# One 2 MB expert weight load in twenty-four is cut into pieces of 112, 8 and 8 partitions

## The chip, the cores and the metric

One NeuronCore of one Trainium2 chip runs the whole program. The metric is the device time of one execution in microseconds (us). The kernel before takes 1229.42 us, the median of three runs (1229.14 to 1229.61). One more execution was recorded by the hardware profiler; all rows below are from it.

## What is computed

One layer of a hybrid decoder for 256 prompt tokens and 8 sample tokens (264 in all, width 1024, float32), and then a final RMSNorm. The layer has a mixer, a cross-attention into 256 memory tokens, and a mixture of experts (MoE), which takes most of the time:

```
logits = xt @ w_router + b_router
top_logit, top_e = lax.top_k(logits, 4)        # 4 of 32 experts for each token
gates = softmax(top_logit)
def expert_ffn(xb, w1, b1, w2, b2):            # w1: 1024 x 2048, w2: 1024 x 1024, one pair an expert
    gu = xb @ w1 + b1
    gate, up = gu[:, :1024], gu[:, 1024:]
    gate = minimum(gate, 7.0); up = clip(up, -7.0, 7.0)
    return ((up + 1) * gate * sigmoid(1.702 * gate)) @ w2 + b2
out = sum over a token's experts of gates * expert_ffn(token)
```

## The kernel before

**Stages.** A front part (memory keys and values, mixer, attention, router) runs over weight chunks of 1 MB. Then PE, DVE and ACT loop over the 32 experts, eight in one pass of their loop (`it`, `j`; `e = 8 * it + j`). For each expert up to 64 tokens are gathered (`xg`), multiplied by its gate/up weights into two PSUM banks (PE line 1170, 64 matmuls), turned (line 1200), biased and passed through SwiGLU on DVE and ACT (lines 863 to 876, 563), and multiplied by the down weights (line 1217, 32 matmuls). The results are put back to their tokens by a product with the gates (`combine`, lines 1144 and 1145).

**Weights.** An expert has 12.6 MB of weights, loaded as six **units** of 2 MB: units 0 to 3 are gate/up (each two k-tiles of 128 rows by 2048), units 4 and 5 are down. One unit fills two neighbouring slots of `ring`, a buffer of 12 slots of 128 partitions x 2048 floats, so the ring holds exactly one expert's six units. In a unit every partition gets 4096 consecutive floats, 16 KB, of DRAM: this is called a **row** below, and a unit has 128 rows. `unit_slot(i)` gives a unit's first slot; each has a semaphore of its own, `landed[s]`, which every load raises by 16.

**Order.** All weight loads are issued by SP (SyncE), in program order, on one queue (`expert_unit`, line 347). Before it overwrites a unit's slots SP waits until PE has used what was in them: `w_used`, raised by PE behind each unit, or `gu_done` behind unit 3 and `d_done` behind unit 5 (`expert_loads`). SP has nothing else to do in this stage. PE waits on `landed[s]` ahead of each unit's first matmul. SP's loop runs over experts 1 to 31 (`Fori(1, NE)`); expert 0's units were issued ahead of it. A further block repeats all experts if one has more than 64 tokens; it does not run here.

The 16 **DMA engines** move the packets of these loads. The profile gives their mean busy share, not which engine moved what.

Of the kernel before, what the change touches and what calls it, by code (L numbers as in the profile page):

```python
# [21 lines left out]
NE = 32  # L22
# [51 lines left out]
def build(nc, x_t, mem_t, w_k, w_v, w_in, w_out, w_q, w_xo, kc, vc, w_gu, w_dn, params, ws_t,  # L74
# [3 lines left out]
    with ExitStack() as ctx:  # L78
# [3 lines left out]
        def sem(name):  # L82
            return ctx.enter_context(nc.semaphore(name))
# [135 lines left out]
        landed = [sem(f"landed{n}") for n in range(RING)]  # L219
        part_landed = [sem(f"part_landed{n}") for n in range(2)]  # L220
        bias_split = sem("bias_split")
        bias_in = sem("bias_in")
        kv_stored = sem("kv_stored")
        mix_stored = sem("mix_stored")
        y_stored = sem("y_stored")
# [81 lines left out]
        def front_uses(slot):  # L307
            return len(range(slot, NF, RING))

        def unit_slot(i):  # L310

            return (NF + 2 * i) % RING
# [10 lines left out]
        @block.sync  # L323
        def _(sp):
            for part, (k, k_end) in enumerate(FIRST_PARTS):
                sp.dma_start(mem_raw[:, k:k_end, :], mem_t[:, k:k_end, :]).then_inc(mem_in[part], 16)
                sp.dma_start(ring[:, 0, 256 * k:256 * k_end], w_k[0, :, 256 * k:256 * k_end]).then_inc(
                    landed[0] if part == 2 else part_landed[part], 16)
            for n, (kind, c) in enumerate(FRONT_CHUNKS):
                if n == 2:  # L330
                    sp.dma_start(resid[:], x_t).then_inc(x_in, 16)
                if n == 0:
                    continue
                if n >= RING:
                    front_free(sp, n - RING)
                sp.dma_start(ring[:, n % RING, :], front_dram[kind][c]).then_inc(landed[n % RING], 16)

            def expert_unit(e, i):
                s = unit_slot(i)
                dst = ring[:, s:s + 2, :].rearrange("p a n -> p (a n)")  # L340
                if i < 4:
                    rows = w_gu[bass.ds(e, 1), 2 * i:2 * i + 2].rearrange("a k p n -> (a k p) n")
                    src = rows.rearrange("(p j) n -> p (j n)", j=ROWS_GU)
                else:
                    rows = w_dn[bass.ds(e, 1), 4 * (i - 4):4 * (i - 4) + 4].rearrange("a k p n -> (a k p) n")
                    src = rows.rearrange("(p j) n -> p (j n)", j=ROWS_DN)
                sp.dma_start(dst, src).then_inc(landed[s], 16)

            for i in range(UNITS):
                front_free(sp, NF - RING + 2 * i)  # L350
                front_free(sp, NF - RING + 2 * i + 1)
                expert_unit(0, i)

            def expert_loads(e, expert):
                for i in range(UNITS):
                    if i == 3:
                        sp.wait_ge(gu_done, e)
                    elif i == 5:
                        sp.wait_ge(d_done, e)
                    else:  # L360
                        sp.wait_ge(w_used, e * 4 - 3 + min(i, 3))
                    expert_unit(expert, i)

            with sp.Fori(1, NE) as e:
                expert_loads(e, e)

            sp.wait_ge(iters_ready, 1)
            end = sp.value_load(iters[0:1, 0:1], min_val=4, max_val=20)
            with sp.If(end > 4):
                with sp.Fori(1, end >> 2) as again:  # L370
                    with sp.Fori(0, NE) as expert:
                        expert_loads(again * NE + expert, expert)
            for m in range(0, KT, 2):
                sp.wait_ge(y_done, m + 2)
                sp.dma_start(y_t[:, m:m + 2, :], resid[:, m:m + 2, :]).then_inc(y_stored, 16)
            sp.wait_ge(y_stored, 16 * KT // 2)
            sp.wait_ge(kv_stored, 32)
            sp.wait_ge(mix_stored, 48)
# [516 lines left out]
        def _(pe):  # L895
# [252 lines left out]
            with pe.Fori(0, end) as it:  # L1148
                for j in range(8):
                    e, i, cur = it * 8 + j, j % 4, (j // 2) % 2  # L1150
                    twin = it * 4 + j // 2

                    def expert_unit(n):
                        s = unit_slot(n)
                        pe.wait_ge(landed[s], e * 16 + 16 * (front_uses(s) + 1))
                        return ring[:, s:s + 2, :].rearrange("p a n -> p (a n)")


                    pe.wait_ge(gu_copied, e + 1)
                    if i % 2 == 0:  # L1160
                        pe.wait_ge(side_copied, twin * 3 + 1)
                    for u in range(4):
                        if j == 0 and u == 2:
                            pe.wait_ge(emptied, NG)
                        w = expert_unit(u)
                        for k in (2 * u, 2 * u + 1):
                            for n in range(2):
                                for h in range(2):
                                    at = SLOT * (k % 2) + D * h + 512 * n
                                    last = mm(ps[64 * h:64 * h + 64, n, :], xg[:, cur, k, SLOTS * (j % 2):SLOTS * (j % 2) + SLOTS],  # L1170
                                              w[:, at:at + 512], start=(k == 0), stop=(k == KT - 1))
                        last.then_inc(w_used if u < 3 else gu_done, 1)

                    pos = twin * 3 + 2 * (j % 2)
                    if i % 2 == 0:
                        pe.wait_ge(side_copied, pos + 1)
                        pe.wait_ge(w_built, twin + 1)
                        for t in range(TT):
                            width = P if t < 2 else NS
                            last = turn(ps[:, 5, P * t:P * t + width], w_hot[0:width, t, :],  # L1180
                                        ident[0:width, 0:width])
                        last.then_inc(side_filled, 1)
                        pos = pos + 1

                    pair = 1 - i // 2
                    if i == 0:
                        pe.wait_ge(y_copied, twin * 2 + 1)
                    if i == 2:
                        pe.wait_ge(y_copied, twin * 2 + 1)
                    biased = j in (4, 5)  # L1190
                    if j == 4:
                        pe.wait_ge(gates_zero, it + 1)
                    for r in range(2):
                        combine(e * 4, r, 4 * (i % 2) + r, pair, biased)

                    pe.wait_ge(gu_copied, e + 2)
                    pe.wait_ge(t_read, e * 2 + 1)
                    for f in range(KT):
                        first = P * ROWS_DN * (f // ROWS_DN) + f % ROWS_DN
                        last = turn(ps[:, 2 + f // 4, P * (f % 4):P * (f % 4) + P],  # L1200
                                    gu_sb[:, first:first + ROWS_DN * (P - 1) + 1:ROWS_DN], ident[:])
                    last.then_inc(t_done, 1)

                    pe.wait_ge(side_copied, pos + 1)
                    pe.wait_ge(p_built, twin + 2)
                    gather(ps[:, 5, :], j % 2).then_inc(side_filled, 1)
                    for r in range(2, 4):
                        combine(e * 4, r, 4 * (i % 2) + r, pair, biased)

                    pe.wait_ge(hid_ready, e + 1)  # L1210
                    pe.wait_ge(y_copied, e + 1)
                    for u in range(4, UNITS):
                        w = expert_unit(u)
                        for k in range(4 * (u - 4), 4 * (u - 4) + 4):
                            for h in range(2):
                                at = D * (k % 4) + 512 * h
                                last = mm(ps[64 * h:64 * h + 64, 4, :], hid[:, k, :], w[:, at:at + 512],  # L1217
                                          start=(k == 0), stop=(k == KT - 1))
                        last.then_inc(w_used if u < UNITS - 1 else d_done, 1)
# [72 lines left out]
```

## Time and profile before

| | us |
|---|---|
| median of three runs | 1229.42 |
| the profiled execution | 1230.66 |
| its span, first to last instruction | 1228.9 |
| expert stage, about | 277 to 1211 of the span |

The profiled execution is 1.2 us above the median, and 1.8 us of it lie outside the span. A window such as 1196:1201 is in us from the start of the span. "DMA share" is the mean busy share of the 16 DMA engines; a packet is counted where it starts, so a share can pass 1.00 a little. In a chain of waits, each line is the start, the length and what was running or awaited.

### The profile page before, as it was taken

The numbers are of one execution on the slowest core, as the hardware profiler recorded it, in microseconds if no ns is written. First come the engines' busy times: TensorE is split into PE (matmuls) and PEld (weight loads), VectorE is DVE, ScalarE is ACT, GpSimd is POOL, SyncE is SP. The second block draws the span as 40 slices with busy tenths as digits, with TensorE's granted clock in tenths as the row PEclk, the third lists the DMA queues.
The fourth block names the chain that finished last, engine by engine and source line by source line (L and its number), as shares of the span: only waits on it lengthen the run. The fifth ranks groups of instructions, "written<-read, shape, count | busy, mean of one in ns | idle before, by whom it ended". The sixth has DMA issues, their size and how long they took to land.

```text
span 1228.9 us, 14979 instructions
## 1 busy us (share of the span) xinstructions
PE 1162.9 (95%) x5977; PEld 628.8 (51%) x5977; DVE 282.8 (23%) x608; ACT 166.0 (14%) x267; POOL 31.9 (3%) x68
## 2 busy tenths in 40 slices
PE   8999999999999999999999999999999899999995
PEld 7888887784444454444344434443444343434443
DVE  5114532342111122121111111111111111111115
ACT  2011011022111111111111111111111111111112
POOL 0000000010000000000000000000000000000000
PEclk9999999999999999999999999999999999999998
DMA  9963434948999999999999999999999999999991
GB/s 365 387 222 138 139 138 175 429 189 331 431 426 428 428 427 427 426 427 427 429 427 427 428 427 428 427 428 427 429 427 428 426 428 427 427 429 427 429 397 57
DMA packets 38703, 458.87 MB, mean 373 GB/s; under 512 B 5841, under 2 KB 6353, under 8 KB 7921
## 3 DMA queue, kind: packets, MB, share of 16 engines
q1 hardware_dynamic: 35712, 454.11, 88.1%
q10 hardware_dynamic: 2928, 3.80, 0.9%
q8 instruction: 54, 0.88, 0.3%
q14 instruction: 9, 0.07, 0.0%
HBM read 454.41 MB, written 3.23 MB: 372 GB/s over the span
## 4 chain that ended last, share of the span: by engine, by line
DMA 44%; PE 29%; DVE 3%; issue 1%; DVEq 0%; ACT 0%; SPq 0%; ACTq 0%
DMA ring<-in_w_gu 44%; PE ps L1170 19%; PE ps L1217 6%; PE ps L1145 1%; DVE arena L863 1%; PE ps L1200 1%; PE ps L1117 1%; DVE arena L873 1%; DVE arena L876 1%; PE ps L1144 0%; DVE arena L870 0%; DVE resid L890 0%; DVE resid L882 0%; DVE ssum L608 0%; PE ps L1180 0%
## 5 line engine op out<-in xcount | busy, mean ns | idle before, releaser
L1170 PE MATMUL ps<-ring,arena 128*64 128x512 f32 x2048 | 457.5, 599 | 36.7 <-DMA ring<-in_w_gu 29.2
L1170 PEld LDWEIGHTS ps<-ring,arena 128*64 128x64 f32 x2048 | 144.9, 138 | 343.8 <-issue 279.4
L1217 PE MATMUL ps<-ring,arena 128*64 128x512 f32 x1024 | 226.8, 595 | 6.3 <-DVE arena L876 6.3
L842 DVE TENSOR_TENSOR resid<-resid,ps 128x264 f32<-128x264 f32 x128 | 51.3, 426 | 722.4 <-PE ps L1145 722.4
L940 PE MATMUL ps<-arena,ring 128*128 128x264 f32 (+1 forms) x800 | 179.2, 386 | 1.4 <-issue 1.0
L940 PEld LDWEIGHTS ps<-arena,ring 128*128 128x128 f32 x800 | 151.6, 190 | 27.3 <-issue 1.6
L1217 PEld LDWEIGHTS ps<-ring,arena 128*64 128x64 f32 x1024 | 70.7, 137 | 146.9 <-issue 130.7
L1117 PE MATMUL ps<-arena 128*128 128x128 f32 x816 | 101.7, 281 | 0.0
L1117 PEld LDWEIGHTS ps<-arena 128*128 128x128 f32 x816 | 99.1, 197 | 0.0
L555 ACT ACTIVATE arena<-ps 128x1024 f32<-128x1024 f32 x32 | 32.8, 1024 | 446.2 <-PE ps L1170 446.2
L1145 PE MATMUL ps<-arena 128*128 128x264 f32 x256 | 72.6, 396 | 0.0
L569 ACT ACTIVATE arena<-ps 64x512 f32<-64x512 f32 x32 | 18.9, 590 | 249.4 <-PE ps L1217 249.4
L1145 PEld LDWEIGHTS ps<-arena 128*128 128x128 f32 x256 | 44.8, 190 | 15.2 <-issue 9.7
L863 DVE TENSOR_TENSOR arena<-ps,par 128x512 f32<-128x512 f32 x64 | 44.0, 688 | 25.9 <-PE ps L1200 25.9
L1200 PEld LDWEIGHTS ps<-ident,arena 128*128 128x128 f32 x256 | 34.7, 207 | 7.4 <-issue 6.3
L1200 PE MATMUL ps<-ident,arena 128*128 128x128 f32 x256 | 36.9, 287 | 1.4
L431 POOL TENSOR_TENSOR arena<-arena,gate 128x384 f32<-128x384 f32 x17 | 14.2, 833 | 879.1 <-PE ps L1180 873.0
L563 ACT ACTIVATE arena<-arena 128x512 f32<-128x512 f32 x32 | 20.2, 630 | 85.2 <-DVE arena L868 85.2
L967 PE MATMUL ps<-ring,arena 128*128 128x256 f32 x128 | 28.0, 379 | 0.0
L967 PEld LDWEIGHTS ps<-ring,arena 128*128 128x128 f32 x128 | 24.3, 190 | 3.3
L876 DVE TENSOR_TENSOR arena<-arena 128x512 f32<-128x512 f32 x32 | 22.2, 692 | 3.3
L565 ACT ACTIVATE arena<-ps 128x512 f32<-128x512 f32 x32 | 19.1, 597 | 27.6 <-PE ps L1117 27.6
(187 smaller groups left out, 433.5 us busy)
## 6 DMA issues: line engine op xcount, KB each, us to landing
ring<-in_w_gu SPq DMA_DIRECT2D x128, 2048.0 KB, 23.8
ring<-in_w_dn SPq DMA_DIRECT2D x64, 2048.0 KB, 20.4
ring<-in_w_in SPq DMA_DIRECT2D x10, 1024.0 KB, 27.2
ring<-in_kc SPq DMA_DIRECT2D x8, 1024.0 KB, 4.7
ring<-in_vc SPq DMA_DIRECT2D x8, 1024.0 KB, 4.8
ring<-in_w_v SPq DMA_DIRECT2D x4, 1024.0 KB, 22.7
ring<-in_w_out SPq DMA_DIRECT2D x4, 1024.0 KB, 4.9
ring<-in_w_q SPq DMA_DIRECT2D x4, 1024.0 KB, 4.8
```

Source lines behind the costliest of these rows:

```text
L555: nc.scalar.activation(gu_sb.rearrange("p (a b) -> p a b", a=2), ps[:, 0:2, :], ACT.Copy).then_inc(gu_copied, 1)
L563: nc.scalar.activation(sig[:], tb[:, :, 0:SLOTS], ACT.Sigmoid, scale=ALPHA).then_inc(sig_ready, 1)
L842: TTN(resid[:, m, :], resid[:, m, :], ps[:, 6 + m % 2, 0:T], ALU.add).then_inc(c_added, 1)
L863: TTN(both[:, :, h, :].rearrange("p (b m) s -> p b m s", b=2), turned[:, :, h, :].rearrange("p (b m) s -> p b m s", b=2), bc(bias, 3, [P, ...
L876: TTN(hid[:], up_v, sig[:], ALU.mult).then_inc(hid_ready, 1)
L940: last = mm(b[:, 0:width], w[:, k, P * (m % 2):P * (m % 2) + P], source(k), start=(k == 0), stop=(k == KT - 1))
L967: last = mm(b[:, 0:256], mem[:, k, P * t:P * t + P], w[:, k, :], start=(k == 0), stop=(k == KT - 1))
L1117: last = mm(b[:, P * part:P * part + P], h_tok[:, t, first:first + ROWS_GU * (P - 1) + 1:ROWS_GU], p_hot[:, t, :], start=(t == 0), stop=(t ...
L1145: mm(ps[:, 6 + m % 2, 0:T], y_hot[:, pair, P * m:P * m + P], g_hot[:, pair, :], start=not biased, stop=True).then_inc(c_filled, 1)
L1170: last = mm(ps[64 * h:64 * h + 64, n, :], xg[:, cur, k, SLOTS * (j % 2):SLOTS * (j % 2) + SLOTS], w[:, at:at + 512], start=(k == 0), stop= ...
L1200: last = turn(ps[:, 2 + f // 4, P * (f % 4):P * (f % 4) + P], gu_sb[:, first:first + ROWS_DN * (P - 1) + 1:ROWS_DN], ident[:])
L1217: last = mm(ps[64 * h:64 * h + 64, 4, :], hid[:, k, :], w[:, at:at + 512], start=(k == 0), stop=(k == KT - 1))
```

## The change

SP's first unit of experts 1, 5, 9, ..., 29 (eight units of 192) is no longer one transfer of 128 partitions. It goes out as rows 112 to 119, then rows 120 to 127, then rows 0 to 111. The two small transfers raise a new semaphore, `tilt_landed`, by 16 each; the large one raises `landed[s]` as before. PE, ahead of the first unit of every expert with `i == 1` (`j` 1 and 5), now waits on `landed[s]` and on `tilt_landed`. The bytes, their source and their place in SBUF are the same. To tell the experts apart SP's loop now covers four experts a pass (seven passes, experts 1 to 28) and three experts are written out behind it.

```diff
-            def expert_unit(e, i):
+            def expert_unit(e, i, uneven=False):
...
-                sp.dma_start(dst, src).then_inc(landed[s], 16)
+                if not uneven:
+                    sp.dma_start(dst, src).then_inc(landed[s], 16)
+                    return
+                for p in (112, 120):
+                    sp.dma_start(dst[p:p + 8], src[p:p + 8]).then_inc(tilt_landed, 16)
+                sp.dma_start(dst[0:112], src[0:112]).then_inc(landed[s], 16)
...
-                    expert_unit(expert, i)
-
-            with sp.Fori(1, NE) as e:
-                expert_loads(e, e)
+                    expert_unit(expert, i, quarter == 1 and i == 0)
+
+            with sp.Fori(0, NE // 4 - 1) as quad:
+                for i in range(1, 5):
+                    expert_loads(quad * 4 + i, quad * 4 + i, i)
+            for e in range(NE - 3, NE):
+                expert_loads(e, e, e % 4)
...
                         w = expert_unit(u)
+                        if i == 1 and u == 0:
+                            pe.wait_ge(tilt_landed, quad * 32 + 32)
```

On SP, at the top of the loop over experts, the kernel before has this for the first two units (`w_used` is PE's count of used units):

```order
L364 ISA
L347 ISA [waits w_used]
L347 DMA ring<-in_w_gu 128x4096
L361 REGISTER_ALU
L347 ISA [waits w_used]
L347 DMA ring<-in_w_gu 128x4096
```

The kernel after has this in the same place, for the first expert of the four in a pass:

```order
L370 ISA
L352 ISA [waits w_used]
L352 DMA ring<-in_w_gu 8x4096
L352 ISA
L352 DMA ring<-in_w_gu 8x4096
L353 REGISTER_ALU
L353 DMA ring<-in_w_gu 112x4096
L367 REGISTER_ALU
L349 ISA [waits w_used]
L349 DMA ring<-in_w_gu 128x4096
```

One DMA has become three behind the same wait; the next unit follows as before.

On PE, at the start of the gate/up matmuls of an expert with `i == 1`, before (the last matmuls of the expert ahead, then the first unit; `landed8` belongs to the last down unit, `landed10` to the first gate/up unit):

```order
L1217 MATMUL ps<-ring,arena 64x512 [waits landed8]
...
L1170 MATMUL ps<-ring,arena 64x512 [waits landed10]
L1170 MATMUL ps<-ring,arena 64x512 x7
```

and after:

```order
L1229 MATMUL ps<-ring,arena 64x512 [waits landed8]
...
L1165 ISA [waits gu_copied]
L1177 ISA [waits landed10]
L1182 MATMUL ps<-ring,arena 64x512 [waits tilt_landed]
```

The wait on `landed10` has moved to an instruction of its own, and the matmul carries the new wait. ACT, DVE and GpSimd run the same instructions in the same order.

## Rows read from the trace of the kernel before

**Rows 1.** The page's second part: each line in 40 slices of the span.

```profile
PE   8999999999999999999999999999999899999995
DMA  9963434948999999999999999999999999999991
GB/s 365 387 222 138 139 138 175 429 189 331 431 426 428 428 427 427 426 427 427 429 427 427 428 427 428 427 428 427 429 427 428 426 428 427 427 429 427 429 397 57
```

**Rows 2.** Chain that ended last: start us, length us, what; its middle and end.

```profile
600.46 3.68 PE ps L1170 x16
604.30 25.57 DMA ring<-in_w_gu
629.91 3.68 PE ps L1170 x16
633.76 25.99 DMA ring<-in_w_gu
659.79 3.68 PE ps L1170 x16
...
1162.99 3.68 PE ps L1170 x16
1166.83 26.14 DMA ring<-in_w_gu
1203.06 7.11 PE ps L1217 x32
```

**Rows 3.** DMA view of 290:1203, the stretch in which the queue is never empty.

```profile
DMA packets 26613, 387.51 MB, mean 424 GB/s; under 512 B 2960, under 2 KB 2960, under 8 KB 2960
q1 hardware_dynamic: 26567, 386.79, 99.7%
q8 instruction: 42, 0.69, 0.3%
```

**Rows 4.** Windows at the end of the last load: length, PEclk, DMA share, GB/s.

```profile
1192.00:1192.50 0.50, 1.00 1.00 426
1192.50:1193.00 0.50, 1.00 0.85 360
1193.00:1193.50 0.50, 1.00 0.92 393
1193.50:1194.00 0.50, 1.00 0.77 328
1194.00:1194.50 0.50, 1.00 0.62 262
1194.50:1195.00 0.50, 1.00 0.69 295
1195.00:1195.50 0.50, 1.00 0.38 164
1195.50:1196.00 0.50, 1.00 0.46 197
1196.00:1201.00 5.00, 1.00 0.51 216
1201.00:1201.50 0.50, 1.00 0.22 66
1201.50:1202.00 0.50, 1.00 0.08 33
```

**Rows 5.** DMA view of 1200:1203: GB/s in 40 slices of 0.075 us; the fetch queue.

```profile
GB/s 437 218 0 0 437 218 437 0 437 218 0 0 218 219 219 0 219 0 0 0 0 0 218 0 0 0 0 0 0 0 0 0 0 0 0 0 0 0 0 0
q8 instruction: 1, 0.02, 2.3%
```

**Rows 6.** DMA issues of the page: form, count, KB each, median us to landing.

```profile
ring<-in_w_gu SPq DMA_DIRECT2D x128, 2048.0 KB, 23.8
```

**Rows 7.** Timeline of SP, the last two groups of issues of weight loads.

```profile
1155.45 11.71 SPq L347 DMA_DIRECT2D ring<-in_w_gu  x4
1177.00 3.77 SPq L347 DMA_DIRECT2D ring<-in_w_dn  x2
```

**Rows 8.** DMA view of 269:272, slices of 0.075 us: one load into 32 partitions.

```profile
GB/s 0 0 0 0 0 0 0 0 0 0 0 0 218 382 273 0 0 55 546 273 1 0 0 0 0 0 0 0 0 0 0 0 0 0 0 0 0 0 0 0
q10 hardware_dynamic: 48, 0.13, 18.6%
```

More of the change, by code:

```diff
@@ L222, in build @@
         bias_in = sem("bias_in")
+        tilt_landed = sem("tilt_landed")
         kv_stored = sem("kv_stored")
@@ L352, in _, with expert_loads @@
                 expert_unit(0, i)
-            def expert_loads(e, expert):
+            def expert_loads(e, expert, quarter):
                 for i in range(UNITS):
@@ L370, in _ @@
                 with sp.Fori(1, end >> 2) as again:
-                    with sp.Fori(0, NE) as expert:
-                        expert_loads(again * NE + expert, expert)
+                    with sp.Fori(0, NE // 4) as quad:
+                        for i in range(4):
+                            expert_loads(again * NE + quad * 4 + i, quad * 4 + i, i)
             for m in range(0, KT, 2):
@@ L1150, in _ @@
                     e, i, cur = it * 8 + j, j % 4, (j // 2) % 2
-                    twin = it * 4 + j // 2
+                    twin, quad = it * 4 + j // 2, it * 2 + j // 4
                     def expert_unit(n):
```

## Prediction

> **What bounds the kernel now.** I read the slices of the page first. From the eleventh slice on the DMA line stands at 9, and the rate at 425 to 431 GB/s up to the 38th slice [rows 1]. PE is busy too, so the chain of waits has to decide. In it a long wait for a gate/up load comes once an expert, followed by 16 matmuls of 3.7 us, and the loads take the rest of each period [rows 2]. From 600.46 to 1162.99 there are 19 experts: 29.61 us each. PE is the follower; what arrives last sets the period.
>
> What does an expert need at the mean rate? Six units of 2.097 MB at 427 GB/s are 29.47 us, 4.91 us a unit. The period is 0.14 us longer. The mean rate is that of 16 engines; the period is that of the engine that ends last, since a unit counts as landed only when its last row is there. So the engines are not level, and fall further apart with every expert.
>
> The end of the last load shows how far. After SP's last issue (1177.00 to 1180.8, [rows 7]) no work is added, so each engine runs dry when its own backlog ends. The share falls from 1.00 at 1192 to 0.46 at 1196, and then stands at 0.51 for five whole microseconds, until it falls to nothing at 1201 to 1202 [rows 4]. Half of 16 is eight: **eight engines are done by about 1195, and eight work on for some seven microseconds more.** The mean gap follows from the areas. From 1192 to 1196 the shares sum to 2.85 us, times 16 is 45.5 engine-us; the late eight take 32 of them, so the early eight stop 1.7 us behind 1192, at 1193.7 on average. Behind 1201 there are (0.22 + 0.08) x 0.5 x 16 = 2.4 engine-us left, of which a fetch has 1.1 [rows 5]: the late eight stop at about 1201.2. The gap is 7.5 us.
>
> Where does it come from? Beside the weights there is one other queue in that stretch, instruction fetches: 42 packets of 16 KB [rows 3], each of which holds an engine for 2.3% of 16 x 3 us = 1.1 us [rows 5]. If only the late eight carry them, that is 5.25 each; 7.5 us of gap would be 1.4 us a fetch, a little over its own 1.1 us. The order of size fits. Which engine takes them no row says.
>
> **The change part by part.**
>
> (1) *What an uneven unit does to the engines.* A row of 16 KB is one packet: 26613 packets less the 2960 small ones, over 387.51 MB, are 16.4 KB each [rows 3]. A unit is 128 rows on 16 engines, 8 each, so a row costs its engine 4.91 / 8 = 0.614 us. The piece of 112 gives 7 rows to each engine. A piece of 8 rows is 8 packets, so at most eight engines get one. If both pieces go to the same eight, these carry 9 rows and the others 7: one row, 0.614 us, moves from one half to the other. The Trainium skill, "DMA: Bandwidth & Descriptors", section "Why a DMA increments its semaphore by 16 and not by 1", says that a transfer of SP runs on the largest number of engines up to 16 that divides its slowest dimension, and on the lowest-numbered ones; by it both pieces would use one and the same half. No transfer in this trace has so few rows, so no row bears it out.
>
> (2) *Sum over the run.* Eight such units: 8 x 0.614 = 4.9 us off one half and onto the other. All eight fall into the stretch with a full queue, so nothing evens it out in between.
>
> (3) *Is 4.9 us the right amount?* Now the single engines count, not the means. The last row of the late half starts in the slice at 1201.65 [rows 5] and ends at 1202.3. The early half's last row: the share at 1194.5 to 1195.0 is 0.69, so it still has work there, and at 1195.0 to 1195.5 it has none [rows 4]; I take 1195.4 for its end. With the late half lightened: 1202.3 - 4.9 = 1197.4. The early half becomes 1195.4 + 4.9 = 1200.3, and is last. **The gain is 1202.3 - 1200.3 = 2.0 us.** The swap is overdone; the ideal would be half of 6.9. That no time comes of the other 2.9 us is what is late next.
>
> (4) *Does PE get it?* The chain ends with the last expert's unit 3 (1166.83 + 26.14 = 1192.97), then PE, DVE and ACT until 1203.06, where the down matmuls begin [rows 2]. Units 4 and 5 have landed by then, at the latest by 1202.3 and some tenths. The chain waits for unit 3's last row, which the same late engine brings, and so moves by the same 2.0 us.
>
> (5) *What is added.* SP issues two DMAs more eight times. A load lands a median 23.8 us behind its issue [rows 6], which is 23.8 / 4.91 = 4.8 units: the queue is nearly five units deep and covers it. If that cover were gone, two issues would cost well under 1 us, eight times. Behind SP's waiting instruction only later loads are queued. PE gets one instruction more on eight experts, at a unit whose rows stand ahead of the one the chain waits for: nothing. Small packets for the semaphores are among the 2960 that leave a unit at 4.91 us: 0.1 us in all. SP's longer program may bring two or three fetches; if they go where the others go, the late half has 2.9 us of new slack: nothing. Sum: -2.0 + 0.1 = -1.9 us, a span of 1227.0, 1228.8 for the profiled execution, and **1227.5 us** against the median.
>
> **The rivals.**
>
> *A (forecast), load shift off the late half:* 1227.5, with 1226.0 to 1229.0 as its own range: the early end is read to 0.4 us, and a fetch more or less on the last engine is 1.4 us.
>
> *B, the wrong half.* The pieces fall on the eight engines that are late already. They decide from the first uneven unit on: +4.9 us, **1234.3**. The trace says that exactly eight are late; nothing says which. Speaking against B: nothing in a row, so it keeps a real chance.
>
> *C, the pieces collide on their way into SBUF.* Each of 16 engines brings 427 / 16 = 26.7 GB/s, all at once, into 128 partitions. If neighbouring partitions share a way in that passes no more than one engine's stream, eight engines that write into eight neighbours at once are slowed: through two such ways a piece takes 4 x 0.614 = 2.46 us in place of 0.61, +1.84 us. An engine takes its rows in order, so its later rows wait too. Sixteen pieces: +29.5 us on one half, which has 2.0 us to spare after the shift: +27.5 us, 1257. The large piece also no longer lies as whole units do; at the worst it would take its 4.9 us twice, eight times, another 39 us: 1296. I take 1275. It decides from 2.0 / 8 = 0.25 us a unit on: a little collision suffices to eat the gain. For it: the one load into 32 partitions moves its 0.13 MB in the eight slices from 269.9 to 270.5, 218 GB/s, about half of 427 [rows 8]. Against it: part of these 0.6 us is the first packet's latency, and single slices reach 382 and 546 GB/s, far more than a limit of half would let through if it bit at once. So a buffer or no limit; I cannot tell. The Trainium skill, "SBUF — State Buffer", section "Door 1: The DMA port swizzle", says that 16 ports serve 128 partitions, and that bandwidth depends on how many of them the partitions reach; by it four engines would write through one port, and this change would be slower. That is rule C, and it speaks against the change; rows 8 agree with it in the mean and not in the peak.
>
> *D, nothing is shifted.* The small pieces go alternately to the two halves, or the late engines are late by position in the queue and not by load: 1229.4.
>
> **How the numbers follow.** A 0.50, B 0.10, C 0.34, D 0.06. A's mechanism is read from the share of 0.51 and needs one free choice (the half) and the absence of C; C has half of rows 8 for it. The bound of 0.2% is 2.5 us, about what a measurement of this kernel can tell from no change: faster is below 1227.0, slower above 1231.9. A's 1.9 us is inside it, and passes it in about a quarter of A. Faster 0.13; same 0.37 + 0.06 = 0.43; slower 0.10 + 0.34 = 0.44. The range runs from 1226.0 up to where C is half covered, 1272: some 0.03 below and 0.16 above it.
>
> **What would show it.** A: after SP's last issue, the plateau of about half share shrinks from five microseconds to two or three (the means would be 1196.3 and 1198.6), and the mean period of an expert is 29.54 instead of 29.61 us. The mean rate stays at 427. B: the plateau grows to some 15 us. C: the share stays near 1 while the rate falls below 427 GB/s behind each first unit of experts 1, 5, 9, ..., since packets take longer. D: rows 4 come again. The size would be wrong if a fetch costs other than 1.4 us or if the number of fetches changes by more than two.

## The result and the profile after

The kernel after takes **1324.58 us** (median of four runs, 1319.51 to 1327.86), the kernel before 1229.51 beside it: a ratio of 1.077, interval 1.0753 to 1.0787, or +95.1 us. The forecast was 1227.5 with a range to 1272. The profiled execution has a span of 1322.8 us.

The page's second part, against [rows 1]: PE's and the DMA engines' busy tenths, the granted TensorE clock, and the rate, in 40 slices of 33 us.

```profile
PE   9999999999998998799969987998899878978995
...
PEclk9999999999999999899989998999899989999998
DMA  9863437769999999999999999999999999999981
GB/s 372 342 223 129 143 144 315 309 190 427 429 427 331 428 428 422 301 428 428 386 310 420 427 384 329 397 424 379 327 397 422 382 363 399 408 363 362 379 364 39
```

The DMA line is at 9 as before, so the engines are still called busy. But the rate, 425 to 431 before, dips every fourth slice: 331, 301, 310, 329, 327, and from there it hardly comes back. The dips have the spacing of the cut units.

Windows of SP (length, PEclk, DMA share, GB/s) around the cut unit of expert 13, issued at 646.6:

```profile
645.00:650.00 5.00, 1.00 0.99 419
650.00:655.00 5.00, 1.00 1.07 429
655.00:660.00 5.00, 1.00 1.00 216
660.00:665.00 5.00, 1.00 1.04 210
665.00:670.00 5.00, 1.00 0.99 177
670.00:675.00 5.00, 0.83 1.01 239
675.00:680.00 5.00, 0.50 0.97 301
680.00:685.00 5.00, 0.99 1.01 390
```

For 20 us all 16 engines are busy (share 1.00) and move half of what they moved before (177 to 239 for 427 GB/s). Busy and half as fast: their packets take twice as long. No engine runs dry in these 20 us; what is slow is the packets themselves.

The chain of waits, start and length, against [rows 2]:

```profile
600.37 25.47 DMA ring<-in_w_gu
625.88 3.68 PE ps L1182 x16
629.71 25.59 DMA ring<-in_w_gu
655.35 3.68 PE ps L1182 x16
659.17 42.11 DMA ring<-in_w_gu
701.33 3.68 PE ps L1182 x16
...
793.91 6.49 PE ps L1182 x16
```

Experts without a cut unit wait 25.5 us as before; the one with it waits 42.11, 17 us more. That is the longest. The long waits behind the other cut units are 34.37, 38.30, 34.40, 33.51, 34.93 and 31.70, and from 734 on the waits next to these are longer too (27 to 31 us). The last line is a second cost. Inside the long wait PE runs out of work, from 670.64 to 676.71. Its granted clock falls to 0.83 and then to 0.50 (1.2 GHz, 675:680 above), and the 16 down matmuls behind that gap take 5.33 us for 3.65. Where such a stretch meets the chain, 16 matmuls that took 3.68 us take 6.49, 6.19 and 5.78, 7.4 us more together.

The DMA view of 290:1300, against [rows 3]:

```profile
DMA packets 26826, 388.90 MB, mean 385 GB/s; under 512 B 3088, under 2 KB 3088, under 8 KB 3088
...
q1 hardware_dynamic: 26780, 388.18, 97.6%
q8 instruction: 42, 0.69, 0.3%
```

The bytes are the same, 388 MB, in 1010 us instead of 913. Fetches are the same 42, so SP's longer program brought none. The weight queue fills 97.6% instead of 99.7%, which with the fetches leaves some 21 us of the 1010 in which the engines, on the mean, have no work. Most of these lie at the end: from 1284 to 1300 the share is 0.09, and from 1286 to 1296 it is 0.07, one engine of 16 that works on alone where [rows 4] had eight. The rest of the loss is mostly slower packets, with some stretches in which engines run dry (1240 to 1250, share 0.70). The large pieces land a median 35 us behind their issue, where [rows 6] has 23.8:

```profile
ring<-in_w_gu SPq DMA_DIRECT2D x120, 2048.0 KB, 25.5
ring<-in_w_gu SPq DMA_DIRECT2D x8, 1792.0 KB, 35.0
```

### The profile page after: what moved, and what is told of

It reads as the page before. It is cut to its first block, busy times and chain, and to the rows that moved or that the text cites. A ratio compares the mean times of both kernels' runs of the same rounds, so it can differ in the third digit from the quotient of the medians.

```text
span 1322.8 us, 14938 instructions
## 1 busy us (share of the span) xinstructions
PE 1185.6 (90%) x5977; PEld 631.0 (48%) x5977; DVE 282.6 (21%) x608; ACT 165.9 (13%) x267; POOL 31.8 (2%) x68
## 4 chain that ended last, share of the span: by engine, by line
DMA 61%; PE 16%; DVE 2%; issue 1%; ACT 0%; SPq 0%; DVEq 0%; ACTq 0%
DMA ring<-in_w_gu 61%; PE ps L1182 13%; PE ps L1229 2%; PE ps L1127 0%; DVE arena L873 0%; PE ps L1212 0%; PE ps L1155 0%; DVE resid L900 0%; DVE arena L883 0%; DVE arena L886 0%; DVE resid L892 0%; DVE ssum L618 0%; DVE rstd L626 0%; DVE arena L880 0%; SPq L349 0%
## 5 line engine op out<-in xcount | busy, mean ns | idle before, releaser
L1182 PE MATMUL ps<-ring,arena 128*64 128x512 f32 x2048 | 475.0, 614 | 100.0 <-DMA ring<-in_w_gu 94.2
L1229 PE MATMUL ps<-ring,arena 128*64 128x512 f32 x1024 | 230.8, 603 | 15.8 <-DMA ring<-in_w_dn 9.6
## 6 DMA issues: line engine op xcount, KB each, us to landing
ring<-in_w_gu SPq DMA_DIRECT2D x120, 2048.0 KB, 25.5
```

## The experiments

The theory to be tested is rival C of the prediction: rows collide on their way into SBUF. Its rivals are the number of transfers, SP's new loop, the load moved onto late engines (rival B), and a pattern in DRAM. All kernels are edits of the kernel after, with PE's wait on `tilt_landed` set to what their loads raise. Each time is set against the kernel before as it ran beside it (medians of 1229.25 to 1229.65 us).

### Not the loop, not the count: c1_loop_only and c2_columns

```diff
-                for p in (112, 120):
-                    sp.dma_start(dst[p:p + 8], src[p:p + 8]).then_inc(tilt_landed, 16)
-                sp.dma_start(dst[0:112], src[0:112]).then_inc(landed[s], 16)
+                sp.dma_start(dst, src).then_inc(landed[s], 16)     # c1; and PE's new wait taken out
```

> The kernel after, with its SP loop over four experts, but every unit is again one transfer of 128 partitions and PE has no new wait. Ways-in theory (neighbouring partitions share a way into SBUF, and a piece whose rows go to few of these ways slows every engine that writes there): nothing collides, 1229.5 us. Count theory (the cost is in the number of transfers, semaphores and issues of SP): 1229.5 us too. Loop theory (SP's longer program or its fetches cost the 95 us): 1324 us. So this run bears on the loop alone.

Measured 1229.22 us, ratio 0.9997 (0.9988 to 1.0007). The loop costs nothing.

```diff
+                for c in (3584, 3840):
+                    sp.dma_start(dst[:, c:c + 256], src[:, c:c + 256]).then_inc(tilt_landed, 16)
+                sp.dma_start(dst[:, 0:3584], src[:, 0:3584]).then_inc(landed[s], 16)
```

> The kernel after, but the same eight units are cut along the free dimension: 128 partitions x 3584 floats, and twice 128 partitions x 256 floats, with the same bytes in each piece (1792, 128, 128 KB), the same semaphores and the same waits. Ways-in theory: every piece reaches all ways as a whole unit does, so 1229.5 to 1231 us. Count theory: three transfers in place of one cost what they cost in the kernel after, 1324 us.

Measured 1230.97 us, 1.0009 (1.0000 to 1.0019), 1.6 us more. Three transfers with the same bytes, semaphores and waits as in the change are nearly free when each covers 128 partitions. Forecast term (5) had 0.1 us for what is added. The small pieces have rows of 1 KB here and of 16 KB in the change, so the 1.6 us is not exactly its term, but either is of no weight beside 95.

### Not the moved load: c3_112_16 and c4_64_64

```diff
+                sp.dma_start(dst[112:128], src[112:128]).then_inc(tilt_landed, 16)    # c4: [64:128]
+                sp.dma_start(dst[0:112], src[0:112]).then_inc(landed[s], 16)          # c4: [0:64]
```

> The kernel after, but the eight units are cut into 112 partitions and 16 partitions, so that all 16 engines should carry 7 + 1 rows, as many as in a whole unit: no load moves from one half of the engines to the other. Wrong-half theory (the 95 us are rows moved onto late engines): 1229.5 us. Ways-in theory: the 16 rows go through few ways and the 112 rows do not lie on the engines as a whole unit's do, so most of the loss stays, 1270 to 1320 us.

Measured 1308.73 us, 1.0647 (1.0619 to 1.0675).

> The kernel after, but the eight units are cut into two halves of 64 partitions, 4 rows for each engine and half. Wrong-half theory: no load moves, 1229.5 us. Ways-in theory: each half reaches only half of the ways if they go by blocks of partitions, so a unit takes up to 4.9 us more, eight times: up to 1269 us; less than in the kernel after, since each way still has only two writers.

Measured 1320.97 us, 1.0753 (1.0717 to 1.0789). Each piece has a multiple of 16 rows. If these are dealt out evenly, which no row shows engine by engine, no engine gets more than another, and nearly the whole loss is there. So it is not the load, for which rival B had only 4.9 us in any case. But the size of c4 is a miss: 39 us were expected, 91.6 came. The window of its cut unit of expert 13 shows why the sum fell short; the stretch of half rate is 20 us long, though the unit itself at half rate would take 9.8:

```profile
655.00:675.00 20.00, 0.96 1.00 214
```

### Large piece or small pieces: d1_only_112 and d2_only_8s

One leaves out rows 112 to 127 of the eight units, the other rows 0 to 111.

```diff
+                sp.dma_start(dst[0:112], src[0:112]).then_inc(landed[s], 16)                # d1, nothing else
+                sp.dma_start(dst[112:120], src[112:120]).then_inc(tilt_landed, 16)          # d2
+                sp.dma_start(dst[120:128], src[120:128]).then_inc(landed[s], 16)            # d2
```

> The eight units load only partitions 0 to 111; rows 112 to 127 are left out (PE multiplies what lay there before). Small-piece theory (the cost is in the two pieces of 8 rows, four engines at one way): without them 8 x 0.614 = 4.9 us less than before, 1224.5 us. Large-piece theory (the 112 rows do not lie on the engines as a whole unit's do, and engines meet at ways all along): most of the 95 us stay, 1270 to 1310 us.

Measured 1305.94 us, 1.0621 (1.0569 to 1.0674), +76.6 us: the large piece alone carries most of the 95 us. By rows alone the run would have taken 4.9 us less than the kernel before, so the surplus is 81.5 us, 10.2 a unit. The rate around its cut unit of expert 13 (650 to 665) is 203, 190 and 170 GB/s at a share of 0.98 to 1.04, the same picture as above.

> The eight units load only the two pieces of 8 rows; rows 0 to 111 are left out. If small pieces cost only their rows (2 x 0.614 us on eight engines, in place of 8 x 0.614 on all): some 30 us less than before, 1195 to 1200 us. If four rows in a row share one way: 2 x 2.46 = 4.9 us a unit, as much as a whole unit, 1229 us. If the small pieces carry the 95 us: 1290 us or more.

Measured 1230.06 us, 1.0005 (0.9995 to 1.0016), as the middle case said. Two pieces of 8 rows, an eighth of the bytes, keep the engine that ends last as long as a whole unit of 128 rows. Both parts of C's sum are seen here apart: the small pieces had been priced right (4.9 us a unit), the large one was the part that was taken for an uncertain extra.

### Only the place in SBUF changed: d3_extra_contig and d4_extra_step4

The units are whole again; two further pieces of 8 rows go to spare space, from the same source rows.

```diff
+                spare = arena[:, h_at:h_at + 2048]
+                for p in (0, 8):                                                            # d3
+                    sp.dma_start(spare[p:p + 8], src[p:p + 8, 0:2048]).then_inc(tilt_landed, 16)
+                for p in (0, 1):                                                            # d4
+                    sp.dma_start(spare[p:p + 29:4], src[8 * p:8 * p + 8, 0:2048]).then_inc(tilt_landed, 16)
                 sp.dma_start(dst, src).then_inc(landed[s], 16)
```

> The eight units are whole again (128 partitions); ahead of each, two more pieces of 8 rows x 2048 floats are loaded from the same unit into spare space, one into partitions 0 to 7, one into 8 to 15. Ways-in theory: eight engines write into two groups of four partitions, 4 x 0.307 us a piece; 16 pieces are 19.7 us for these engines, of which 6.9 us are slack if they are the early half: 1242 us (1249 if they are the late half), more if others are held up with them. If only rows count: 16 x 0.307 = 4.9 us, hidden in the early half (1229.4) or not in the late half (1234.3).

Measured 1241.23 us, 1.0098 (1.0082 to 1.0115), +11.9 us: beside the 1242 of the ways-in theory. That figure held for eight early engines, though, and the next run says that two of the eight are late. With a late one among them the same sum gives 1249. So a piece with 8 KB a row costs a late engine about 11.9 / 16 = 0.74 us here, not 1.23. That is still more than its rows (0.31), but that the time came out beside 1242 is in part luck, and the size stays open.

> As the run with contiguous extra pieces, with the same source rows and bytes, but the 8 rows go to every fourth partition: 0, 4, ... 28, and then 1, 5, ... 29, so that each row lies in a group of four partitions of its own. Ways-in theory: no two engines meet, so only the rows count: 1229.4 us if the eight engines of such a piece are the early half, 1234.3 us if they are the late half, and so this run also tells which half the small pieces of the change load. Source theory (the loss comes from how rows are read from DRAM): the same time as with contiguous partitions.

Measured 1233.77 us, 1.0035 (1.0023 to 1.0048). The same bytes from the same rows by the same number of transfers are 7.5 us cheaper when every row goes to a group of four partitions of its own. And the 4.4 us that are left speak of the second question, which engines a piece of 8 rows loads. The end of its last load, in windows of SP, against [rows 4]:

```profile
1194.00:1196.00 2.00, 1.00 0.92 393
1196.00:1198.00 2.00, 1.00 0.86 369
1198.00:1200.00 2.00, 1.00 0.59 254
1200.00:1201.00 1.00, 1.00 0.62 262
1201.00:1204.00 3.00, 1.00 0.19 76
1204.00:1205.00 1.00, 1.00 0.12 49
```

Before, eight engines (0.51) worked on by themselves for five microseconds. Here the share at 1196 is 0.86: most of the early half has been loaded and goes on. But at the end two engines are alone (0.12 of 16), and they end the load. That is what one sees if the eight engines of such a piece are neither the early half nor the late one, but about six early and two late ones. d2 ends in the same way: two engines alone from 1192.5 to 1196 (share 0.13). No single row names an engine, so the numbers six and two are read from the shares.

### Destination or source: f3_even_odd, g1_dst_blocks, g2_src_blocks

```diff
+                sp.dma_start(dst[1:128:2], src[1:128:2]).then_inc(tilt_landed, 16)          # f3
+                sp.dma_start(dst[0:127:2], src[0:127:2]).then_inc(landed[s], 16)            # f3
```

> The eight units are cut into the 64 odd partitions and the 64 even ones, 4 rows for each engine and half as in the run with two blocks of 64, which took 1321 us. Ways-in theory: each half now reaches every group of four partitions and so every way, and two engines that meet alternate between two ways: 1240 to 1270 us. Source or shape theory (any transfer of fewer than 128 partitions is slow, wherever its rows go): 1321 us again.

Measured 1229.80 us, 1.0001 (0.9991 to 1.0011). Two halves of 64 partitions cost 91.6 us as blocks and nothing as odd and even ones. Better than expected, and by itself not a proof, as the source rows changed with the partitions. The next two part them; g1 has `dst[64:128] <- src[1:128:2]` and `dst[0:64] <- src[0:127:2]`, g2 has `dst[1:128:2] <- src[64:128]` and `dst[0:127:2] <- src[0:64]`.

> The eight units are cut into two halves of 64 rows; the odd rows of DRAM go to partitions 64 to 127, the even rows to 0 to 63 (so PE multiplies permuted weights in these units). Destination as in the run with two blocks of 64 (1321 us), source as in the run with odd and even rows (1230 us). Ways-in theory (the loss arises where the rows enter SBUF): 1321 us. Source theory (it arises in the pattern in which rows are read from DRAM): 1230 us.

Measured 1318.29 us, 1.0716 (1.0669 to 1.0763).

> The counterpart: rows 64 to 127 of DRAM go to the odd partitions, rows 0 to 63 to the even ones (permuted weights again). Source as in the run with two blocks of 64 (1321 us), destination as in the run with odd and even rows (1230 us). Ways-in theory: 1230 us. Source theory: 1321 us.

Measured 1229.23 us, 0.9998 (0.9986 to 1.0009). The page's rates in 40 slices show the two side by side, g1:

```profile
GB/s 372 341 226 130 135 153 307 310 190 427 426 428 336 427 428 427 317 428 428 397 330 427 427 366 345 427 427 346 347 428 428 331 320 428 425 338 307 420 375 42
```

and g2:

```profile
GB/s 369 391 215 138 139 137 188 427 178 342 429 426 428 429 427 426 425 427 430 427 428 427 428 427 427 427 429 427 427 427 429 426 427 428 427 428 427 428 401 61
```

For these halves the partitions written decide, not the rows read. The Trainium skill, "SBUF — State Buffer", section "Door 1: The DMA port swizzle", gives the map: 16 ports, two groups of four neighbouring partitions to a port, and the two halves of 64 partitions on different ports. A block of 64 reaches half the ports, the odd partitions reach all. The trace agrees: half the rate (214 GB/s, c4) with blocks, 427 without.

The swap was made for halves of 64 only. By the same map a block of 112 reaches every port, so counting ports does not explain the 76.6 us of d1. That there, too, several engines write through one port at a time fits the same signature (share near 1, rate near 200 GB/s), but no run took source and place apart for that piece.

### A price that grows: f1_first_only and f2_last_only

In the seven units that are not cut, SP loads the whole unit and raises `tilt_landed` by 32 itself. In f1 the loads of experts 1 to 4 are also written out ahead of SP's loop.

```diff
+                if uneven == 2:
+                    sp.sem_inc(tilt_landed, 32)
-                if not uneven:
+                if uneven in (0, 2):
```

> Only the first of the eight units (expert 1) is cut into 112, 8 and 8 partitions; the other seven are whole. Fixed-price theory: each cut unit costs 95 / 8 = 11.9 us, so 1241 us. Skew theory (a cut unit slows all engines for as long as some engine is still in it, so its price grows with how far the engines have drifted apart, and at expert 1 they have drifted by about 1 us only): the dip in the rate there is worth some 3 to 4 us in the trace of the kernel after, so 1232 to 1234 us.

Measured 1233.66 us, 1.0034 (1.0021 to 1.0047): +4.0 us. From 262 to 310 us the DMA engines moved 12.28 MB here and 13.65 MB in the kernel before. The difference is 3.2 us of the full rate, most of the price.

> Only the last of the eight units (expert 29) is cut; the other seven are whole. Fixed-price theory: 1241 us. Skew theory: the engines are 8 us apart there as in the kernel before, so more than at expert 1: 1240 to 1244 us. The difference between this run and the run with the first unit alone is what tells the two theories apart: none by fixed price, 8 us or so by skew.

Measured 1244.04 us, 1.0119 (1.0102 to 1.0136): +14.4 us. The same cut costs 4 us at expert 1, where by the skew theory the engines are nearly level, and 14 at expert 29, where they are some seven or eight microseconds apart. A fixed price of 11.9 is out. The rate shows where it comes from: from 1104 to 1130, 26 us, it is 215 GB/s at a share of 1.01 (c1 has 429 there), 12.9 us of the full rate lost. In f1 it is back at 425 from 294 on, some 14 us behind the issue. That it is the drift that makes the slow stretch longer was argued ahead of the run and fits; the place in the run was changed, not the drift by itself. There is a second difference: at expert 1 PE does not yet wait for loads (in the chain of the kernel before no load is awaited until 457). It explains little, since the loads themselves lost only 3 to 4 us there.

### The shift without blocks: h1_spread_tilt8, h2_spread_even, h3_spread_tilt6

```diff
+                for p in (0, 8):                                                            # h1
+                    sp.dma_start(dst[p:p + 113:16], src[p:p + 113:16]).then_inc(tilt_landed, 16)
+                sp.dma_start(dst[4:125:8], src[4:125:8]).then_inc(tilt_landed, 16)          # all three
+                sp.dma_start(dst[2:127:4], src[2:127:4]).then_inc(tilt_landed, 16)
+                sp.dma_start(dst[1:128:2], src[1:128:2]).then_inc(landed[s], 16)
```

h2 has two pieces `[0:121:8]` of half the columns in place of the pieces of 8; in h3 the second half of the columns goes as 6, 6 and 4 rows.

> The load shift of the change without its blocks. The eight units are cut into the 64 odd partitions, the 32 of the form 4n + 2, the 16 of the form 8n + 4, and twice 8 partitions of the form 16n and 16n + 8. So eight engines get one row more and eight one less per cut unit, as in the change, but no piece is a block. By the forecast's own term (the eight engines of an 8-row piece are the early half): 1227.5 us, with 1 to 2 us for the added transfers 1228.5 to 1229.5. By the reading of the run with extra pieces at every fourth partition (two of these eight engines are late ones): 8 x 0.614 = 4.9 us more, 1234 to 1236 us. If a piece of 8 is slow wherever its rows go: 1240 us or more.

Measured 1259.80 us, 1.0246 (1.0222 to 1.0270).

> Control for the other two: as many pieces (64, 32, 16 partitions, and 16 partitions in two halves of 2048 floats), each with a multiple of 16 rows, so that every engine keeps its load. Ways-in theory and load theory: 1229.5 us and 1 to 2 us for four transfers more in eight units, 1230 to 1231.5 us. A price of 0.3 us or more for each added transfer would give 1239 us.

Measured 1258.09 us, 1.0223 (1.0198 to 1.0248). The control missed by 27 us, so this group doesn't decide what it was made for.

> As the control, but the second half of the 16 rows (2048 floats each) goes out as 6, 6 and 4 rows. If such a piece runs on the lowest-numbered engines and the early six of the lowest eight are the lowest six: four engines get 2 half rows more, two get 1 more, ten get 1 less per cut unit; late engines 8 x 0.307 = 2.5 us less, the early ones at most 4.9 us more, so 2 us gained against the control: 1228 to 1229.5 us. If a late engine is among the lowest four, 4.9 us are lost against the control: 1235 us.

Measured 1261.94 us, 1.0263 (1.0242 to 1.0283). No shift beats its control: +1.7 and +3.9 us with intervals of the ratios that overlap. The fault was probably in my pieces: 16 partitions of the form 8n + 4, or 8n, lie in every second group of four only. By the map in the Trainium skill, "SBUF — State Buffer", section "Door 1: The DMA port swizzle", each set reaches half of the ports, and the 29 us of h2 agree with that, but no run took these pieces apart, and against the number of transfers (five or six for one) as the cause there is only c2 (three for one, 1.6 us).

## Why the prediction was wrong

**The mechanism that decided was in the text, as rival C, with a chance of 0.34.** The step of the forecast that failed is the price of the pieces in (1) and (5). There a row costs its engine 0.614 us wherever it is written, a piece of 8 rows costs its rows, and the whole cutting 0.1 us; slower packets were put at nothing. The runs show otherwise. The two pieces of 8 hold an engine for 4.9 us a unit and not 1.2 (d2), the piece of 112 costs 76.6 us in eight units (d1), and g1 against g2 shows for halves of 64 that the partitions written make the difference (1318.3 and 1229.2 us).

The 0.50 for A against 0.34 for C came from the weighing of [rows 8]. The load into 32 partitions had moved 218 GB/s on the mean, half of 427, and I set against it that single slices reached 382 and 546. A slice of 75 ns with packets counted where they start says nothing of a limit behind a buffer, so the peaks should have had no weight. But the mean is weak evidence too. The load is over in 0.6 us with the first packet's latency in it, and the load of 2 MB into all 128 partitions that ran just before it, alone, moved 350 GB/s from 263 to 269 and not 427. The agreement with the 214 GB/s of c4 may be chance. Nothing in [rows 8] spoke for giving the absence of C the larger half.

**C's price was too low as well** (27 to 67 us, 95 measured). The small pieces were right: 4.9 us a unit (d2). The large piece was put at 0 to 4.9 us a unit above its rows; alone it costs 76.6 / 8 = 9.6, which is 10.2 above its rows (d1). And the sum took a cut unit as if all engines went through it together. The half rate lasts 20 us, not 10 (c4), and the price goes from 4.0 to 14.4 us (f1, f2). My explanation is that the engines are up to eight microseconds apart, so that some are in the cut unit while others are in whole ones and write through the same ways; no run changed the drift alone. Nor did C have a term for PE's clock, 7.4 us on the chain, or for engines that run dry.

**Steps (1) and (2), the load shift.** As long as rows do not collide, a row at 0.614 us and 4.9 us for eight of them hold: d4 adds 4.9 us of rows to eight engines and takes 4.4 us more. But the eight engines are not the early half. I gave two cases, the right half (A) and the wrong one (B); what the shares of d4 and d2 show is a mix. So A's gain of 2.0 us would most likely not have come without collisions either: two late engines would have got the eight extra rows. That was not shown in a run of its own, since h1 to h3 collide.

**Step (3), the plateau,** was read rightly: c1, which is the kernel before with another loop, has it again (0.47 at 1196 to 1201). That instruction fetches cause it was not tested. **Step (4),** that PE follows the last row, holds: the waits in the chain carry the loss. **Step (5)** holds for the issues and the fetches (c2; 42 fetches before and after); its 0.1 us for the cutting is what failed.

The row for C in "What would show it" did name the picture that came: share near 1, rate below 427 behind each cut unit.

No version came out that beats the kernel before; f3, g2 and c1 are level with it.

## What to carry to other kernels

A transfer that covers part of the partitions has to be judged by which partitions it covers: at full load 64 odd ones are as fast as 128, and a block of 64 or 112 lowers the rate of everything in the queue to about half for 14 to 26 us. Where the share of the DMA engines stays at 1.00 and the rate falls, look for writers that meet, not for a missing load. A fast peak in a short load is no reason to put such a meeting at nothing: time one cut unit first. And before load is moved from a late engine to an early one, find out which engines a transfer runs on: a share gives how many are late, not which.

## What the chip did that was not expected

Eight of 16 DMA engines end about 7 us behind the others, in the kernel before and in c1, where every unit is whole. The engines do not run level even there, and hardly more than 42 instruction fetches of 16 KB stand beside the weights. Why is open.

Cutting a unit into odd and even partitions cost nothing measurable (1229.80 against 1229.65 us), although each half has half the partitions.

One cut unit of 2 MB among 192 halves the rate of the queue for up to 26 us (f2), as long as five whole units take, and costs 4.0 us early in the run and 14.4 us late.
